# Cross attention issued between its query and output projections, and the index keys and index weights computed in one output tile

## The reference, cut to what matters

```
def memory_cross_attention(hn, mem, g_mem, w_q, w_k, w_v, w_o):
    q = (hn @ w_q).reshape(b, s, 4, 128)          # 512 queries
    k, v = (m @ w_k), (m @ w_v)                   # 256 memory tokens, 4 heads of 128
    p = softmax(einsum("bshd,bmhd->bhsm", q, k) * 128**-0.5)
    o = einsum("bhsm,bmhd->bshd", p, v)
    return o @ w_o                                # added to h, then squared-relu MLP
```

## Time and profile before

| | us |
|---|---|
| median of 3 runs | 2126.75 |
| lowest and highest run | 2126.26, 2127.61 |
| the profiled execution | 2119.47 |
| its span in the trace | 2117.7 |
| PE busy in the span | 2019.0 |
| DVE, ACT, POOL busy | 1064.5, 750.4, 227.0 |

### The profile page before, as it was taken

How to read it: one execution, slowest core, us unless ns; L and a number is a source line. 1 busy time by engine, 2 the same in 40 slices (tenths; PEclk the granted TensorE clock), 3 DMA queues, 4 the chain that set the end, 5 groups by cost and what they waited for, 6 DMA issues and landing times.

```text
span 2117.7 us, 28559 instructions
## 1 busy us (share of the span) xinstructions
PE 2019.0 (95%) x11514; PEld 1727.5 (82%) x11514; DVE 1064.5 (50%) x1388; ACT 750.4 (35%) x947; POOL 227.0 (11%) x191
## 2 busy tenths in 40 slices
PE   7999888999999999999899999999997899999996
PEld 6778656688888887999899999999885588888885
DVE  6668755544444554121543434345797543443434
ACT  4448734532231434223332122224434442222122
POOL 2011011200000130012200000002145120000001
PEclk9999999999999999999999999999998999999998
DMA  4225111122222221111122222222121022222221
GB/s 171 100 80 99 73 40 60 60 100 99 96 84 100 89 90 60 60 60 41 60 80 99 90 90 94 86 97 85 71 85 61 15 85 100 99 82 96 99 99 60
DMA packets 27792, 174.68 MB, mean 82 GB/s; under 512 B 4385, under 2 KB 4513, under 8 KB 7730
## 3 DMA queue, kind: packets, MB, share of 16 engines
q1 hardware_dynamic: 25680, 167.32, 21.8%
q0 software_dynamic: 1856, 5.90, 1.6%
q10 hardware_dynamic: 162, 0.10, 0.0%
HBM read 168.53 MB, written 4.78 MB: 82 GB/s over the span
## 4 chain that ended last, share of the span: by engine, by line
PE 68%; issue 20%; DVE 6%; ACT 4%; POOL 2%; DMA 1%; SPq 0%; POOLq 0%; DVEq 0%; ACTq 0%
PE lin L447 56%; PE aux L2171 1%; POOL squares L628 1%; PE aux L1283 1%; ACT w_hi L362 1%; PE aux L1740 1%; PE aux L1754 1%; DVE w_lo L369 1%; PE lin L1238 1%; PE lin L2141 1%; PE aux L2155 1%; DMA w_raw<-in_weights 1%; PE aux L1267 1%; PE aux L1768 1%; PE aux L2019 0%
## 5 line engine op out<-in xcount | busy, mean ns | idle before, releaser
L447 PE MATMUL lin<-v_hi,w_hi 128*128 128x264 f32 (+1 forms) x1712 | 573.8, 335 | 4.9 <-DVE v_lo L613 3.4
L447 PE MATMUL lin<-v_hi,w_lo 128*128 128x264 f32 (+1 forms) x1712 | 570.8, 333 | 0.0
L447 PE MATMUL lin<-v_lo,w_hi 128*128 128x264 f32 (+1 forms) x1712 | 569.4, 333 | 0.0
L447 PE MATMUL lin<-x_hi,w_hi 128*128 128x512 f32 (+1 forms) x1176 | 416.6, 354 | 17.7 <-DVE tmp L541 6.6
L369 DVE TENSOR_TENSOR w_lo<-w_raw,w_hi 128x2048 fp32r<-128x2048 f32 (+1 forms) x144 | 328.4, 2281 | 188.8 <-ACT w_hi L362 188.6
L447 PE MATMUL lin<-x_hi,w_lo 128*128 128x512 f32 (+1 forms) x1176 | 413.1, 351 | 0.0
L447 PE MATMUL lin<-x_lo,w_hi 128*128 128x512 f32 (+1 forms) x1176 | 412.5, 351 | 0.0
L362 ACT ACTIVATE w_hi<-w_raw 128x2048 fp32r<-128x2048 f32 (+1 forms) x155 | 292.9, 1890 | 286.1 <-PE lin L447 274.4
L447 PEld LDWEIGHTS lin<-v_hi,w_hi 128*128 128x128 f32 x1712 | 324.4, 189 | 40.5 <-DVE v_lo L613 4.4
L447 PEld LDWEIGHTS lin<-v_lo,w_hi 128*128 128x128 f32 x1712 | 324.3, 189 | 33.6 <-issue 0.7
L447 PEld LDWEIGHTS lin<-v_hi,w_lo 128*128 128x128 f32 x1712 | 324.2, 189 | 32.1
(11 more groups left out here) (373 smaller groups left out, 2353.1 us busy)
## 6 DMA issues: line engine op xcount, KB each, us to landing
w_raw<-in_weights SPq DMA_DIRECT2D x155, 1024.0 KB, 4.8
rel_by_distance<-tmp POOLq DMA_DIRECT2D x1, 2620.0 KB, 57.3
rel_bias<-rel_by_distance POOLq DMA_DIRECT2D x8, 264.0 KB, 2.9
h<-in_x_t SPq DMA_DIRECT2D x4, 512.0 KB, 8.1
out_t<-h SPq DMA_DIRECT2D x4, 512.0 KB, 2.8
o_t<-in_mem_t POOLq DMA_DIRECT2D x1, 1024.0 KB, 5.2
cst<-in_consts SPq DMA_DIRECT2D x1, 512.0 KB, 9.7
col<-in_cols ACTq DMA_DIRECT2D x1, 67.0 KB, 5.7
```

The source lines that it names most:

```text
L447: last = nc.tensor.matmul(o, a, b, start=(k % (L.kc // k_banks) == 0 and p == 0), stop=((k + 1) % (L.kc // k_banks) == 0 and p == 2))
```

## The change

In cross attention the helper calls for `XQ` disappear: `pe_cross`, `act_cross` and `dve_cross` now issue the four query tiles themselves, with logits and transposes of earlier heads between them, and the first unit of `XO` (four tiles) after it, in pieces by head: its first two tiles take heads 0 and 1, then 2, then 3, its last two tiles take all four heads at once. Logits of head 2 come ahead of the last query tile. Odd heads' logits move to PSUM banks 1 and 3, the results of the heads to banks 0, 2 and the first two of `aux`. The row maxima of a head become two instructions over half of it each. The split of `XO`'s second unit moves into the stage, so `dve_residual` and `act_residual` leave it out (`splits_from=1`). The load of the Exp table moves ahead of a weight split.

In layer `kw` the 64 keys and the 8 weights share one tile (partitions 0 to 63, and 64 to 71); its second tile is gone. ACT copies the weights first; DVE waits for that and then scales the keys twice, once to each half of `ki_t`. All later tiles change their place in PSUM from one of the two to the other.

```diff
-    ("kw", 1, 8, 2, T2, False), ("qi", 2, 8, 2, S1, False), ("c", 1, 8, 2, T2, False),
+    ("kw", 1, 8, 1, T2, False), ("qi", 2, 8, 2, S1, False), ("c", 1, 8, 2, T2, False),
...
         def pe_cross(pe):
-            wait_taken(pe, XQ)
+            w_unit = XQ.unit0
+
+            def query(t):
+                unit, m = w_unit + t // 2, t % 2
...
+                slot, before, _ = XQ.tile(t // 2, m, 0)
+                pe.wait_ge(sem("w_lo_ready"), unit + 1)
+                pe.wait_ge(sem(f"lin_taken{slot}"), before)
...
             def logits(hd):
+                slot, before, _ = XQ.tile(hd // 2, hd % 2, 0)
+                pe.wait_ge(sem(f"lin_taken{slot}"), before + 1)
                 if hd >= 2:
                     pe.wait_ge(sem("xa_exp"), hd - 1)
...
+            def mix(hd):
                 pe.wait_ge(sem("xa_pt"), hd + 1)
                 if hd >= 2:
-                    pe.wait_ge(sem("xa_lo"), hd - 1)
+                    pe.wait_ge(sem("xa_exp"), 3)
...
+            def output(t, heads):
...
+                for k in heads:
+                    pe.wait_ge(sem("xa_lo"), max(k + 1, 2))
...
+            query(0)
+            pe_squares(pe, l_xa)
+            query(1)
+            logits(0)
+            query(2)
+            logits(1)
+            turn(0)
+            logits(2)
+            query(3)
+            turn(1)
+            logits(3)
+            mix(0)
+            mix(1)
+            turn(2)
+            output(0, (0, 1))
+            output(1, (0, 1))
+            mix(2)
+            turn(3)
+            output(0, (2,))
+            output(1, (2,))
+            mix(3)
+            output(0, (3,))
+            output(1, (3,))
+            for t in range(2, 4):
+                output(t, (0, 1, 2, 3))
+            pe_linear(pe, XO, x_hi, x_lo, first_unit=1)
...
         def act_cross(act):
...
+            next_hi(act, XQ, 0, 0)
+            act_root(act, l_xa)
+            nc.scalar.preload_act_table(ACT.Exp)
+            next_hi(act, XQ, 1, 0)
             exp(0)
+            turned(0)
             exp(1)
-            for hd in range(4):
-                turned(hd)
-                if hd + 2 < 4:
-                    exp(hd + 2)
-                output(hd)
+            exp(2)
+            turned(1)
+            output(0)
+            exp(3)
+            output(1)
+            turned(2)
+            split_hi(act, XO.unit0 + 1, 0, XQ.tiles_end)
+            output(2)
+            turned(3)
+            output(3)
...
         def dve_cross(dve):
...
+            next_lo(dve, XQ, 0, 0)
+            dve_root(dve, l_xa)
+            taken(0)
+            taken(1)
             maxima(0)
+            next_lo(dve, XQ, 1, 0)
+            normalized(0)
+            taken(2)
             maxima(1)
-            normalized(0)
...
+            maxima(2)
+            normalized(1)
+            taken(3)
+            normalized(2)
+            maxima(3)
+            output_lo(0)
+            output_lo(1)
+            normalized(3)
+            split_lo(dve, XO.unit0 + 1, 0, nc.vector)
+            output_lo(2)
+            output_lo(3)
...
-            slot, _, n = KW.tile(0, 1, 0)
+            slot, before, n = KW.tile(0, 0, 0)
             act.wait_ge(sem("lin_done"), n + 1)
-            nc.scalar.activation(half(wi_row[:, :]), lin[slot][0:8, :, 0:HALF], ACT.Copy, scale=W_IDX_SCALE)\
-                .then_inc(sem(f"lin_taken{slot}"), 1)
+            nc.scalar.activation(half(wi_row[:, :]), lin[slot][64:72, :, 0:HALF], ACT.Copy, scale=W_IDX_SCALE)\
+                .then_inc(sem("wi_row"), 1)
...
-            nc.vector.tensor_tensor(half(ki_t[:, :]), psum_tile(slot, T2), half(scale_d[:, :]), ALU.mult)\
-                .then_inc(sem(f"lin_taken{slot}"), 1)
+            dve.wait_ge(sem("wi_row"), 1)
+            for r in (0, 64):
+                ins = nc.vector.tensor_tensor(half(ki_t[r:r + 64, :]), lin[slot][0:64, :, 0:HALF],
+                                              half(scale_d[0:64, :]), ALU.mult)
+            ins.then_inc(sem(f"lin_taken{slot}"), 1)
```

More of the change, by code:

```diff
@@ L510, in build, with dve_residual @@
                            "a_out", "dn1a", "dn1b", "dn1c"]
-        def dve_residual(dve, L, scale=None, N=None, after=None, scale2=None, after_first=None):
+        def dve_residual(dve, L, scale=None, N=None, after=None, scale2=None, after_first=None, splits_from=0):
             base = KD * residual_layers.index(L.name)
             def unit(j, i):
-                next_lo(dve, L, j, i)
+                if not (is_first(j, i) and splits_from):
+                    next_lo(dve, L, j, i)
                 if after is not None and is_first(j, i):
@@ L550, in dve_residual, with act_residual @@
             for_units(dve, L, unit, N is not None)
-        def act_residual(act, L, N, after=None):
+        def act_residual(act, L, N, after=None, splits_from=0):
             base = KD * residual_layers.index(L.name)
             def unit(j, i):
-                next_hi(act, L, j, i)
+                if not (is_first(j, i) and splits_from):
+                    next_hi(act, L, j, i)
                 if after is not None and is_first(j, i):
@@ L1487, in logits, with turn @@
                 for t in range(4):
-                    mm = nc.tensor.matmul(cross_logits(hd)[:, t, :], xq_t[:, hd, t * P:t * P + P], xk_t[:, hd, :],
+                    mm = nc.tensor.matmul(cross_logits(hd, t), xq_t[:, hd, t * P:t * P + P], xk_t[:, hd, :],
                                           start=True, stop=True)
                 mm.then_inc(sem("xa_logits"), 1)
-            logits(0)
-            logits(1)
-            for hd in range(4):
+            def turn(hd):
                 pe.wait_ge(sem("xa_p"), hd + 1)
@@ L1502, in pe_cross @@
                 mm.then_inc(sem("xa_turned"), 1)
-                if hd + 2 < 4:
-                    logits(hd + 2)
+            def mix(hd):
                 pe.wait_ge(sem("xa_pt"), hd + 1)
                 if hd >= 2:
-                    pe.wait_ge(sem("xa_lo"), hd - 1)
+                    pe.wait_ge(sem("xa_exp"), 3)
                 for b in range(2):
-                    mm = nc.tensor.matmul(lin[1][:, hd % 2, :], xv_tok[:, b, hd * P:hd * P + P],
+                    mm = nc.tensor.matmul(cross_out(hd), xv_tok[:, b, hd * P:hd * P + P],
                                           xp_t[:, hd % 2, b, :], start=(b == 0), stop=(b == 1))
                 mm.then_inc(sem("xa_out"), 1)
+            def output(t, heads):
+                unit, m = XO.unit0 + t // 4, t % 4
+                w = [x[:, unit % 2, :].rearrange("p (k n) -> p k n", k=4) for x in (w_hi, w_lo)]
+                slot, before, _ = XO.tile(t // 4, m, 0)
+                pe.wait_ge(sem("w_lo_ready"), unit + 1)
+                pe.wait_ge(sem(f"lin_taken{slot}"), before)
+                for k in heads:
+                    pe.wait_ge(sem("xa_lo"), max(k + 1, 2))
+                    for p, (wp, xp_) in enumerate(((w[0], x_hi), (w[0], x_lo), (w[1], x_hi))):
+                        mm = nc.tensor.matmul(lin[slot][:, 0, :], wp[:, k, m * P:m * P + P], xp_[:, k, 0:S1],
+                                              start=(k == 0 and p == 0), stop=(k == 3 and p == 2))
+                if heads[-1] == 3:
+                    mm.then_inc(sem("lin_done"), 1)
+            query(0)
[24 more added lines that the diff above has]
+            pe_linear(pe, XO, x_hi, x_lo, first_unit=1)
         def act_cross(act):
-            nc.scalar.preload_act_table(ACT.Exp)
             def exp(hd):
@@ L1520, in exp @@
                 for t in range(4):
-                    x = nc.scalar.activation(xp[:, hd % 2, t, :], cross_logits(hd)[:, t, :], ACT.Exp,
+                    x = nc.scalar.activation(xp[:, hd % 2, t, :], cross_logits(hd, t), ACT.Exp,
                                              bias=x_stat[:, hd, 1, t:t + 1], scale=XA_SCALE,
@@ L2413, in _ @@
             act_residual(act, WB, l_xa, after=lambda: act_root(act, l_sb))
[L2414 removed]
             act_cross(act)
[L2416 removed]
+            act_residual(act, XO, l_ff, splits_from=1)
             for part in "abcd":
@@ L2544, in _ @@
                       after={(0, 0): lambda: pe_squares(pe, l_sb)})
-            pe_linear(pe, XQ, v_hi, v_lo, ready=lambda k: l_xa.wait_operand(pe, k),
-                      after={(0, 0): lambda: pe_squares(pe, l_xa)})
             pe_cross(pe)
-            pe_linear(pe, XO, x_hi, x_lo, ready=lambda k: pe.wait_ge(sem("xa_lo"), max(k + 1, 3)))
             for part in "abcd":
```

53 lines of the change are left out of this document (31 added, 22 removed).

## The result

The changed kernel takes **2111.87 us** (median of 5 runs, 2111.05 to 2116.69) against 2126.26 for the kernel before beside it (5 runs, 2122.64 to 2127.61). The ratio is 0.995, with a 95% interval of 0.9933 to 0.9967, so a gain of 7.0 to 14.2 us; the forecast was 10.6. The same kernel, timed once more beside before, gave 2115.66 (12 runs) against 2120.81 (23 runs), ratio 0.997, 0.996 to 0.9981: 4.0 to 8.5 us. The forecast lies inside the first interval and outside the second, so there is something to explain although the range held the time. The medians differ by 14.4.

The account below looks back on a forecast made before the run. PE's instruction stream was taken to set the time. Cross attention 5.6 plus index keys and weights 5.0 gave 10.6 us, so 2126.75 - 10.6 = 2116.2 us, with a range of 2111.5 to 2121.5.

Parts of the forecast that it names:

- Cross attention, 5.6 us: Cross attention: new waits sum to 3.8 us against 9.3 idle before; the output projection ends at 400.4, not 406.00.
- The wait of 0.3 before output tile 2: Cross attention's output projection: PE idles 0.3 us until DVE has taken output tile 0.
- 9.4 idle, not 9.3: Cross attention before the change: 27.2 us from query to output projection, 17.8 of work, so 9.3 us idle.
- Rivals A and D: Clock falls: A after each new cross attention wait, 2121.3, chance 0.13; D through the woven stretch 343 to 400, slower, 0.03.
- Rival B: Cross attention: round trips stay mostly exposed, its gain near 0, index part alone, 2121.8; chance 0.07.
- the three waits: Cross attention: PE waits for split head results of about 1.2, 0.65 and 1.6 us.
- Rival E: ACT or DVE hand over sooner than summed and the exposed waits halve: 2113; chance 0.06.
- Index layer, 5.0 us: Layer kw loses 48 matmuls, 5.8 us of PE's path, less 0.8 us of new waits.
- The two small waits: Index queries (QI): PE idles 0.3 us for the keys' PSUM place at tile 1 and 0.5 at tile 2.
- I see no event there pinned to absolute time: Between QI and attention: search, POOL splits and transfer follow earlier work by fixed lags, so the gain reaches the end.
- Rival C: Removed index tile does not reach the end: search, POOL or bias transfer holds attention's start; 2121.2, chance 0.07.
- My sum takes none: TensorE's clock: no falls counted, though a wait may bring one, costing about 1.7 us of matmul time.

Follow-up runs that it names:

- kw_only: The index layer part alone (keys and weights in one tile), cross attention as before; 2119.74 us against 2120.81 for before, ratio 0.9992.
- before_warm: The kernel before, with PE's waits for normalized exponentials in attention filled by matmuls whose result is overwritten; 2114.18 us against 2121.57 for before.
- the filling: Matmuls whose result the transposes overwrite, put in PE's waits for normalized exponentials in attention; in the changed kernel 2107.23 us, ratio 0.993.
- xa_only: The cross attention part alone, index keys and weights in two tiles as before; 2113.45 us against 2120.81 for before, ratio 0.9964.
- after: The changed kernel in its first timing and profile; 2111.87 us against 2126.26 for before, ratio 0.995.
- norm7: The changed kernel with the norm of the latents after 7 rounds of the search instead of 8; 2113.16 us, ratio 0.996.
- parity: The changed kernel, layer kw still counted as two tiles so later tiles keep before's PSUM places; 2120.07 us against 2123.39 for before, ratio 0.9994.
- xorder: The changed kernel, PE's head 3 value products ahead of head 2's output matmuls and ACT's head 1 rounding before head 3's exponentials; 2106.73 us, ratio 0.9935.
- after_again: The changed kernel timed and profiled once more; 2115.66 us against 2120.81 for before, ratio 0.997.
- norm7_warm: The changed kernel with PE's attention waits filled with matmuls and the latents' norm one search round earlier; 2103.90 us against 2121.57 for before.
- warm_again: Second timing of the changed kernel with PE's attention waits filled with matmuls; 2106.94 us against 2121.57 for before, ratio 0.993.

## Why the prediction was right, and where it was not

**Cross attention, 5.6 us: right, wait by wait.** From the first logits to the next layer 57.0 us against 56.9 forecast; waits 1.22, 0.63, 1.50 and 1.27 against 1.2, 0.65, 1.6 and 1.5; no wait for exponentials. The wait of 0.3 before output tile 2 did not come, so the waits are 0.6 less than forecast, and the work between them is 0.7 more (52.4 against 51.7). Two slips in the working changed nothing: its figures give 9.4 idle, not 9.3, and 2.8 us are two half tiles, not four. Rivals A and D fall: PEclk is 1.00 from 340 to 400 us in both profiles of the changed kernel. Rival B falls: the three waits came to 3.35 us, not 10.2. Rival E's 2113 is nearer to the first median, 2111.87, than the forecast is, but its condition, waits halved, was not met. One thing was not in the sum: the old order lost the clock in kw_only and before_warm (80.0 in place of 76.9 us) and the new one did not in eleven profiles, so the part is worth up to 8.6.

**Index layer, 5.0 us: 4.6 measured** from `kw` to `a_out`. The two small waits came as 0.22 and 0.46, against 0.3 and 0.5.

**"I see no event there pinned to absolute time": this step failed.** The argument was that the search and POOL's splits both follow QI's last tile by fixed lags. They start together, but the search runs on DVE's time and the splits on PE's. With the search's first rounds 1.1 us longer in sum, a pair of DVE instructions that had just been ahead of a split started 0.26 behind it and took 4.2 longer; with the filling that costs attention 4.2 us. Rival C named the search among what could hold attention's start, but for the removed tile, and there it is wrong: the collision stands in xa_only and not in kw_only. kw_only's time, 1.1 us below before, is what rival C asks for, yet attention's bias work began 4.6 us earlier against the start of `kw`; in its profile the gain went to the clock.

**"My sum takes none" of the clock: right in cross attention, wrong for attention.** I looked for falls where the change was, and found none there. But attention had 24 us at the lower level in before, and my sum took these as given. They are not a constant: 34 us in after. Here the Trainium skill (TensorE: Matmul & The Clock Gate, HAM oscillation) warned that bursts divided by waits keep losing the full clock. The page's own case has waits of some 3 to 5 us for a transfer; the prediction stretched it to the new waits of cross attention, 0.6 to 1.5 us, where the clock stayed at 1.00. In attention the trace agrees with it (0.66 in 1590 to 1610 us of after, around PE's idle 7.3 and 2.4 us).

So 10.6 was the right size for what the change does to PE's path, and the measured gain is that less what attention takes back, which differs from execution to execution: 4.0 to 14.2 us over the intervals of the two comparisons. That the first comparison shows as much as 14.4 between medians owes something to before's median there, 2126.26, the highest of the four comparisons (2120.81, 2123.39 and 2121.57 in the others).

**Left open.** What decides how often the clock falls in attention: without the filling, after, norm7, parity and kw_only have 145.0 to 145.5, and before, xa_only and xorder 136.4 to 137.5, with nothing between; neither the collision nor the shared tile sorts them (xorder has both and is short), and all but the changed kernel have one profile each. And why a round of the first search loop takes 4.0 us in place of 3.88 in every kernel with the new cross attention, xa_only too, and in none with the old: the trace of after has a new wait of DVE for itself, of 0.2 us, before the first replacement of each round; the loop's code is the same.

```profile
DVE scores L2160 <- DVE best L2155: 2.0, 8, 0.5
```

## What to carry to other kernels

A gain at one stage is only banked when the next stage with idle gaps has been passed: cut both traces at instructions that they share and compare the lengths, the untouched ones too. When work on two engines is not joined by a semaphore, look for pairs that just miss each other in the trace of before; a shift of 1 us can cost 4. Where TensorE loses its clock in a stage full of waits, filling these waits with matmuls that nobody reads can pay: it gained 7.4 us in the kernel before and, by the ratios, 4 to 8 in the changed one, but nothing clear of noise in xa_only.

## What the runs showed of the hardware that I had not expected

- A DVE scalar_tensor_tensor of 128x528 takes 0.76 us alone and 4.93 when it starts 0.26 us after a GpSimd subtraction of 4.62 us has begun (profile of after). Where it starts 0.9 us ahead, the subtraction takes 5.08 (profile of before).
- Equal code with nearly equal waits was granted 1.00 in one execution and 0.86 and 0.84 in two others (the old cross attention, 360 to 380 us of before, kw_only and before_warm).
- 24 us at the lower level cost attention 7.5 us (before against before_warm). Removing a delay of 4.3 us ahead of attention gave 0.5 us of attention in the profile with the clock free (2.5 between medians, norm7 against after_again) and 4.2 with the filling (3.0 between medians, norm7_warm against warm_again).
